# Score matmuls of the mixing layers at 128 contraction rows instead of 96

## The reference

```
# differential attention: 4 heads x 2 halves, 32 features each
s = einsum('bqhcd,bkhcd->bchqk', q_blk, k) * scale + bias
p = softmax(s);  a = p[:, 0] - lam * p[:, 1]
o = einsum('bhqk,bkhd->bqhd', a, v)

# latent attention: 4 heads, 64 plain features and 32 rotated ones
s = einsum('bqhd,bkhd->bhqk', qn, k_nope) + einsum('bqhd,bkd->bhqk', qr, k_rope)
p = softmax(s * scale)
```

## Time and profile before

| | |
|---|---|
| three runs, us | 1138.37, 1137.87, 1137.67 (median 1137.87) |
| the profiled execution, us | 1138.59 |
| its span (first to last instruction), us | 1136.8 |
| busy share of the span | PE 99%, PEld 86%, DVE 69%, ACT 47%, POOL 5% |
| mean granted TensorE clock | 0.999 of full speed |
| transfers | 207.02 MB, 182 GB/s on average |

### The profile page before, as it was taken

One profiled execution on the slowest core, in us unless ns is written; L12 is line 12 of the kernel. 1 busy time (PEld: TensorE's weight loads), 2 busy tenths in 40 slices (PEclk: granted clock), 3 DMA queues, 4 the chain that ended last, 5 costly groups with the idle time before them and its releaser, 6 DMA issues. The chain is left out here.

```text
span 1136.8 us, 16893 instructions
## 1 busy us (share of the span) xinstructions
PE 1121.8 (99%) x6556; PEld 974.8 (86%) x6556; DVE 782.1 (69%) x1015; ACT 533.3 (47%) x702; POOL 60.5 (5%) x99
## 2 busy tenths in 40 slices
PE   8999999999999999999999999999999999999997
PEld 7888888898888888879988888888899988888886
DVE  6766666767667666677676676666766866766665
ACT  5533333456653334344585533343446755333332
POOL 1000000000000000003400000000034000000000
PEclk9999999999999999999999999999999999999999
DMA  8766566664356565668733465656676244665550
GB/s 254 254 209 196 178 202 202 221 207 142 118 167 222 185 188 182 209 156 249 205 122 114 165 222 186 187 184 209 176 238 157 85 149 133 215 208 185 184 184 37
DMA packets 170295, 207.02 MB, mean 182 GB/s; under 512 B 20707, under 2 KB 153187, under 8 KB 170242
## 3 DMA queue, kind: packets, MB, share of 16 engines
q1 hardware_dynamic: 166226, 202.89, 55.8%
q0 software_dynamic: 4016, 3.42, 1.6%
HBM read 201.98 MB, written 1.16 MB: 179 GB/s over the span
## 5 line engine op out<-in xcount | busy, mean ns | idle before, releaser
L657 ACT ACTIVATE whi<-raw 128x2048 fp32r<-128x2048 f32 x176 | 336.4, 1915 | 382.6 <-PE bank L1572 245.5
L971 DVE TENSOR_TENSOR wlo<-raw,whi 128x2048 fp32r<-128x2048 f32 x171 | 391.9, 2294 | 158.3 <-ACT whi L657 158.2
L1568 PE MATMUL bank<-h_both,whi 128*128 128x512 f32 x1280 | 304.6, 390 | 0.0
L1568 PEld LDWEIGHTS bank<-h_both,whi 128*128 128x128 f32 x1280 | 237.7, 188 | 47.7
L1542 PE MATMUL bank<-whi,o_hi 128*128 128x512 f32 x448 | 176.2, 393 | 0.0
L1543 PE MATMUL bank<-wlo,o_hi 128*128 128x512 f32 x448 | 174.9, 390 | 0.0
L1544 PE MATMUL bank<-whi,o_lo 128*128 128x512 f32 x448 | 174.4, 389 | 0.0
L1572 PEld LDWEIGHTS bank<-h_both,wlo 128*128 128x128 f32 x1280 | 164.1, 191 | 6.2
L1572 PE MATMUL bank<-h_both,wlo 128*128 128x256 f32 x1280 | 166.0, 283 | 0.0
L1544 PEld LDWEIGHTS bank<-whi,o_lo 128*128 128x128 f32 x448 | 84.1, 188 | 17.9
L1542 PEld LDWEIGHTS bank<-whi,o_hi 128*128 128x128 f32 x448 | 84.3, 188 | 17.6 <-issue 1.3
(11 more groups left out here) (200 smaller groups left out, 1280.7 us busy)
## 6 DMA issues: line engine op xcount, KB each, us to landing
raw<-in_w_gate_up SPq DMA_DIRECT2D x44, 1024.0 KB, 5.1
raw<-in_w_down SPq DMA_DIRECT2D x44, 1024.0 KB, 4.9
raw<-in_w_gate SPq DMA_DIRECT2D x22, 1024.0 KB, 5.4
raw<-in_w_up SPq DMA_DIRECT2D x22, 1024.0 KB, 5.4
raw<-in_w_in SPq DMA_DIRECT2D x20, 1024.0 KB, 6.3
raw<-in_w_o SPq DMA_DIRECT2D x12, 1024.0 KB, 5.1
raw<-in_w_kv SPq DMA_DIRECT2D x8, 1024.0 KB, 5.3
raw<-in_w_q SPq DMA_DIRECT2D x4, 1024.0 KB, 5.0
```

The costliest lines, as they stand in the source:

```text
L657: act.activation(whi[:, s, :], raw[:, s, :], ACT.Copy).then_inc(hi_ready, 1)
L971: dve.tensor_tensor(wlo[:, s, :], raw[:, s, :], whi[:, s, :].bitcast(F32), ALU.subtract).then_inc(lo_ready, 1)
L1568: pe.matmul(bank[bk + jj][:, :], hi[:, kc, jj * P:(jj + 1) * P], h_both[:, kc, :, :].rearrange("p a t -> p (a t)"), start=(kc == 0), stop= ...
```

## The change

The differential stacks get a fourth band, so that a matmul over 128 rows also adds lo*lo. That makes 32 instead of 24 transfers a layer, and PE waits for 16 x 32 a layer. The latent matmuls also take all 128 rows of `qall`; rows 96 to 127 of both operands hold zeros, which POOL writes once, after MoBA's last scores and FFN 1's norm. PE waits for that write before item 0.

```diff
@@ load_diff
                 pool.wait_ge(diff_low, 2 * l + n - 3)
-                to, order = (o_lo, (diff_hi, diff_hi, diff_lo)) if n == 5 else (o_hi, (diff_hi, diff_lo, diff_hi))
+                to, order = (o_lo, (diff_hi, diff_hi, diff_lo, diff_lo)) if n == 5 else (o_hi, (diff_hi, diff_lo, diff_hi, diff_lo))
                 for b, part in enumerate(order):
                     for r in range(4):
                         first, second = DIFF_SLOT[r], DIFF_SLOT[r + 4]
@@ POOL's program
             for v in range(4):
                 rsqrt(v)
+            pool.wait_ge(scores, 16)
+            pool.wait_ge(rstd_ready, tile_no(3, 1) + 1)
+            pool.memset(qall[MLA_D:P, :, :], 0.0).then_inc(rows_zero, 1)
+            pool.wait_ge(rows_zero, 1)
@@ PE, scores of a mixing layer
                         if i == 0:
+                            pe.wait_ge(rows_zero, 1)
                             pe.wait_ge(mla_copied, l + 1)
                             pe.wait_ge(mla_rope, 4 * l + 4)
                         if i < 4:
-                            q, kk = qall[0:MLA_D, i, :], qall[0:MLA_D, 4 + i, :]
+                            q, kk = qall[:, i, :], qall[:, 4 + i, :]
@@
                             if g == 1:
-                                pe.wait_ge(diff_in, 16 * 24 * (l + 1))
-                                q, kk = o_hi[0:96, DIFF_SLOT[i - 8], :], o_lo[0:96, DIFF_SLOT[i - 8], :]
+                                pe.wait_ge(diff_in, 16 * 32 * (l + 1))
+                                q, kk = o_hi[:, DIFF_SLOT[i - 8], :], o_lo[:, DIFF_SLOT[i - 8], :]
```

More of the change, by code:

```diff
@@ L287, in bass_two_stacks @@
         na_ready = sem("na_ready")
+        rows_zero = sem("rows_zero")
         diff_low, diff_in = sem("diff_low"), sem("diff_in")
```

## The result

With the change the kernel takes 1139.68 us, the median of 22 runs (1139.17 to 1141.0), and before 1138.34 in 22 runs beside them (1137.45 to 1140.39). The ratio of the times is 1.0012, with a 95% interval of 1.0006 to 1.0017: slower by 1.4 us, between 0.7 and 1.9. That is less than the 0.2% (2.3 us) for which the chances were given, and still clear of nothing. The profiled execution took 1140.61, its span is 1138.8 us against 1136.8 before.

What follows compares the result with a forecast made beforehand. PE, busy 99% of the span, was taken to bound the kernel. Matmuls and borders, transfers, waits and zeros each counted 0, so the runs' median of 1137.87 us gave 1137.9, range 1136.7 to 1139.6.

Steps and rivals of the forecast that it cites:

- the matmuls and the borders: Score blocks of both layers: 128-row matmuls last as long as 96-row ones, at most 0.08 us more; taken as 0.
- the 24 borders: Switches between 96 and 128 rows, two for each of 12 score blocks: gain at most 0.24 us, taken as 0.
- the 0.12 us of the earlier trace: Cost of leaving the 64-column value products; a rival charged it to each 96-row border: 2.9 us faster, 1135.0, chance 0.04.
- the transfers land in time: Eight more POOL transfers a layer: worst landing 576.8 us, 2.2 before PE's first differential scores at 578.97; cost 0.
- the power of line 629: POOL's step behind the transfers, waiting 34.77 us for DVE; 4.3 us more of issues would leave it 30.
- the zeros and the waits: POOL's write near 327 us beside DVE's norm: 0 to 0.4 us; PE's two waits: at most 0.1; both taken as 0.
- the lower bound of 3.3: Shorter estimate of POOL's zeros write, 16 rows of 204 ns each: 3.3 us; the longer was 7.9 us.
- The range's upper end of 1139.6: Highest run 1138.37 plus 0.4 us for the zeros, 0.1 for the waits and 0.7 for the runs' spread.
- The rivals: Borders drain, 1135.0 us, chance 0.04; key stack lands late, 1140.5, 0.06; zeros block DVE, 1140.3, 0.02.
- the stack that lands late: Rival: POOL's queue lags with sixteen transfers, PE waits before differential scores, 1.3 us a layer: 1140.5 us, chance 0.06.
- a wait of line 1841: Sign that the forecast is wrong: PE's differential score line, numbered as in the changed kernel, waits on a transfer.
- the base: Starting time of the forecast, the earlier runs' median of 1137.87 us, to which terms of 0 were added.

Runs made afterwards that it cites:

- the kernel with this half alone: The kernel before plus only the zeros, PE's wait for them and 128-row latent scores, with 24 transfers a layer: 1138.32 us, ratio 1.0001.
- the four drained kernels that were run eleven times: Early POOL drain: kernel before, layer 1, 1137.7 us; both layers, 1137.41; layer 1 plus seven identity matmuls in PE's wait, 1137.57; changed kernel, layer 1, 1137.66.
- the wait filled to 0.52 us: Kernel before with the layer 1 drain, plus seven unused identity matmuls where PE waits 2.1 us for ACT in layer 0: 1137.57 us, ratio 0.9995.

## Why the prediction was wrong, and where it was right

**Right: the matmuls and the borders.** 379 and 302 ns, a step of 0.56 us, no gain from the 24 borders, and the same 550.5 us of PE from the first differential scores to its last matmul. The Trainium skill's page TensorEngine Tiling (Array Packing), section Key Properties, has a change of the tiling mode drain the engine. Taken to hold for these borders, at the 0.12 us of the earlier trace rows each, it would have given 2.9 us back; the trace shows no such drain between 96 and 128 rows.

**Right: the transfers land in time.** The last issue was forecast for 571.4 on the old trace. It came at 572.1, of which 0.7 is PE's shift in that trace; of 2.2 us to spare 2.1 are left. Not foreseen was that the landings would get longer, 4.5 us in the median instead of 2.7, but the worst of the key stack hardly moved, 5.5 in layer 0 and 5.9 in layer 1 instead of 5.4. One reading was off without a consequence: the power of line 629 (now 630) was to be left a wait of 30 us, and it has 32.4. The sum had taken off the issues of both stacks, 4.3 us, though four of the eight fill a pause of POOL between them, as the same paragraph had found.

**Right: the zeros and the waits.** 1.81 us, below the lower bound of 3.3; DVE lost 0.01 us, PE's wait nothing, and the kernel with this half alone is at 1.0001. By the Trainium skill's page SBUF — State Buffer, section Who interferes with whom, a GpSimd instruction that only writes doesn't hold up DVE's operation with two inputs in SBUF. The trace agrees, with 1.42 against 1.41 us for the one beside nearly the whole write and 2.29 against 2.28 for the one beside its last 0.57 us.

**Wrong: "What stands behind the transfers on POOL is the power of line 629 [...] So the eight transfers cost 0 as long as the 2.2 us last".** The list of what stands behind them on POOL stopped one item short: behind the last power stands the program's closing drain, and its length grows with each transfer issued. That term was put at 0 and is 16 x 0.082 = 1.31 us, which is the difference of the medians (1.34) and the centre of the ratio (1.4). None of the cover counted for it, since it isn't paid when the transfers run but when the program ends. And it lay on the path in full: of the 4.9 us of POOL's drain in the kernel before, 4.2 ran beside the last norm and store, and 0.7 already stood open behind SP. So nothing was left to hide any part of 1.31 us more.

It was there to be read. The drain isn't in the page's busy shares, and the chain of waits of the kernel before ends with DVE's closing at 1133.7, 3.1 us before the end of the span. What shows it is the view of the closing line, which I had not opened. With the 4.925 us of that row and 52 transfers the upper bound would have been 4.925 / 52 = 0.095 us a transfer, 1.5 us for sixteen, 1139.4 from 1137.9. The range's upper end of 1139.6 was built from other terms, none of which came. The rivals had no case for the drain either. The nearest, the stack that lands late, looked for the loss where the transfers land, and would have shown a wait of line 1841, which there is not.

**A smaller miss: the base.** The forecast started from 1137.87, the median of three runs; 22 runs beside the changed kernel have 1138.34. With the drain's 1.31 us the first gives 1139.18, still inside the range, and the second 1139.65. So it is the drain that made the kernel slower, and the 0.5 us by which the three runs lay low that carried the time of 1139.68 past 1139.6. In the other direction there was luck: the forecast of less than 0.2% of change came true only because the term left out, 0.12%, happened to be smaller than that.

**Not of the change:** the 1.3 us at the lower clock and the 0.5 us of the start phase in the profiled execution. Taken alone, the two spans (+2.0) would have misled by half.

**A version below both.** The kernel before with an early drain of POOL, in layer 1, in layer 0 or in both, ran at 1137.0 to 1137.7, and the changed one with it at 1137.66. Against the changed kernel that is a clear gain of some 2 us. Against the kernel before each interval alone still holds 1.0, so no single comparison shows a gain; the four drained kernels that were run eleven times agree on 0.6 to 0.8 us, and the profile gives 0.7.

## What to carry to other kernels

Before adding transfers to POOL's own queue, open the view of the program's closing line and see which engine's last instruction ends when: if it is POOL's drain, each transfer costs its 0.08 us wherever it was issued and however well it was hidden. A drain put behind the last transfer, where POOL is idle anyway, takes that cost off the end. And a difference of two spans has to be split along the same instructions before it is given to the change: here a third of it was the clock's and the start's.

## What the runs showed of the hardware

- POOL's drain takes 0.11 us, plus what is left of the running instruction (a reading from the fit, behind powers of 0.55 and 1.66 us), plus 0.082 us for each transfer that POOL issued since its last drain: 0.657 us for none, 4.925 for 52, 6.232 for 68, 8.845 for 100. It makes no difference whether a transfer moves 128 bytes or half a megabyte, or whether it landed 1100 us ago. SP's closing drain, behind over 200 transfers of SP's, took 13 ns.
- PE's clock fell to 1.2 GHz for some 3.5 us behind PE's 2.1 us wait near 510 us, or behind the next one, in eight of the eleven traces of kernels that have this wait; seven times it cost PE 0.1 us or nothing, once 1.3 us. With the wait filled to 0.52 us it did not fall there.
- The first 15 us of the program differ by up to 2.1 us from trace to trace, and what is won or lost there stays to the end. In two traces with a late start ten matmuls took 4.3 us instead of 2.56 at a granted clock of 1.00. The first ten of the program took 3.9 to 4.6 us in all twelve.
